# Scaling q and k on VectorE, the output gain moved to the gate, and another spread of the convolution taps

## The chip, the cores and the metric

The kernel runs on one core of one Trainium2 chip. The metric is the device time of the whole program in microseconds (us). Five engines matter: TensorE (PE in the rows: matmuls and transposes), VectorE (DVE), ScalarE (ACT), GpSimd (POOL) and the queue that issues the weight loads (SP). Each works through its own list of instructions in a fixed order, and waits on semaphores for the others.

## The reference

The reference is a stack of transformer blocks over 256 tokens of width 1024 in float32: two layers with attention and a convolution-gated feed-forward part, and then a block of another kind. The change touches the middle of that last block, a gated delta rule of 8 heads of 128 channels, which runs beside a long convolution:

```
c = depthwise_conv(glu_a * sigmoid(glu_b), conv_dw_w) + conv_dw_b          # 31 taps, 1024 channels
qkv = silu(depthwise_conv(concat(q, k, v), qkv_conv_w))                    # 5 taps
q = l2_norm(q) * (HEAD_DIM_2 ** -0.5)
k = l2_norm(k)
o_fwd = gated_delta_rule(q, k, v, g[:, :, 0], beta[:, :, 0])
o_bwd = rev(gated_delta_rule(rev(q), rev(k), rev(v), ...))
o = rms_norm(o_fwd + o_bwd, delta_norm_g) * silu(z)                        # gain of 128 numbers, the same for all heads
y_delta = o @ w_delta_out
```

## The kernel before

All weights are streamed from memory in slots of 1 MB. Each slot is split in two parts, a rounded one (whi, by ACT) and its remainder (wlo, by DVE or POOL), and every product is three matmuls on them (L981 to L983). That is most of TensorE's work.

The delta rule is laid out by hand as ten rounds of eight ticks. One half of a weight slot (24 matmuls, in two parts of 12) fills each tick for TensorE as long as the round has slots: rounds 0 to 5 have four (all eight ticks), round 6 three, round 7 two (ticks 0 to 3), round 8 three, round 9 four. Between these parts stand the steps of three heads at once: in round r the head r is prepared (its q, k and v), head r-1 has its triangular systems inverted, and head r-2 is finished.

- Inversion: ticks 1 to 6 each make one level. TensorE multiplies (L1318), DVE masks the product into `prod` (L2415), TensorE multiplies that (L1348, L1350), ACT copies the two results (L1806, L1808). L1318 stands at the start of the tick, L1348 behind the first 12 matmuls of the slot. Tick 7 is a check with L2421 in the place of L2415, and `solved` (L2433), for which TensorE waits at L1370.
- Preparation: in tick 3 TensorE turns q and k (L1261), and ACT takes four sums of squares (L1756). In tick 4 POOL makes reciprocal lengths of them (L919 twice, then the power L920), and ACT scales the four 128x128 pieces with them (L1761). In tick 5 TensorE turns them back (L1271). In tick 6 the decay ratios are started (L2383), in tick 7 they meet the products.
- Slots that end are evacuated by ACT and DVE at the start of the next even tick: for q, k and v eight taps of the short convolution (L2308, two groups of four around the other steps of the tick), for z the gate (`xn`, L2324), for the long convolution its input (L2319).
- The long convolution is 8 channel tiles of 31 taps each on DVE (L2363, L2368 and L2371), with a closing sum (`cacc`, L2375) for each tile. A table says how many taps each tick takes (`TAP_COUNT`: for even rounds 8, 6, 0, 5, 0, 3, 7, 4, for odd ones 8, 6, 0, 5, 3, 4, 6, 3). Half of a tick's taps stand before the steps of preparation, half behind.
- The halves of a slot's wlo that are made in ticks 4 and 5 are DVE's (L1989), the others POOL's (L939).

DVE's order within a tick is: `prod` of the level, evacuation part 0, the gate of the short convolution, taps part 0, the steps of preparation and finish, evacuation part 1, the wlo half, taps part 1.

The output's gain (`delta_norm_g_2`) is applied after round 9, when the outputs have been turned so that channels are rows: ACT multiplies by it while rounding (L1594, four times), and DVE does so for the remainders (L2025, four times).

## Time and profile before

| | |
|---|---|
| time, median of 3 runs | 1378.86 us (1376.05 to 1382.32) |
| the profiled execution | 1378.86 us, of which the span is 1377.0 |
| TensorE busy | 1322.1 us, 96% of the span |
| DVE busy | 860.5 us, 62% |
| ACT busy | 702.3 us, 51% |
| POOL busy | 194.2 us, 14% |
| mean granted TensorE clock | 0.982 |
| DMA, mean | 145 GB/s |

Shares are over the whole span. The stretch from the first decay values to the end of round 7 is 697 to 1010 us; in it TensorE is busy for 298.0 of 313 us, DVE for 240.1, ACT for 188.0. A row of the order of time gives start, length, engine, line, operation, tiles and shapes, count, and in brackets the idle time of the engine before it with what ended it. Rows with a count are merged, so that the length is from the first start to the last end. DVE's instructions overlap at their edges by about 0.08 us, so a length is that much longer than the step to the next one.

### The profile page before, as it was taken

The page shows a single profiled execution, that of the slowest core. Times are in us where ns is not written, and L with a number is a line of the kernel's source. Part 1 is how long each engine was busy: PE and PEld are TensorE (multiplying, and loading weights), DVE is VectorE, ACT ScalarE, POOL GpSimd, SP SyncE. Part 2 cuts the span into 40 slices and gives each one's busy share as a digit, 9 for nine tenths or more (in the row PEclk, how much of TensorE's full clock was granted, in tenths as well). Part 3 has the DMA queues.
Part 4 walks back from the last instruction along what each step waited for, and adds up shares of the span by engine and source line. Part 5 has one row for each costly group of instructions (what it writes and reads, how often), then busy time and mean ns, then how long its engine had stood idle before and what let it go on. Part 6 is the DMA issues. An engine that isn't in the chain of part 4 may idle for free.

```text
span 1377.0 us, 22043 instructions
## 1 busy us (share of the span) xinstructions
PE 1322.1 (96%) x9030; PEld 1207.6 (88%) x9030; DVE 860.5 (62%) x1468; ACT 702.3 (51%) x1154; POOL 194.2 (14%) x175
## 2 busy tenths in 40 slices
PE   8998999999999999999989999999888999999996
PEld 7776799998877799998889999999788989999875
DVE  6773578873654478885358787877734445555355
ACT  4553455553446555554266566666546335444343
POOL 2000000000000000000135535444422201000001
PEclk9998999999999999999999999999998999999998
DMA  7623155545433245555443233233102445455531
GB/s 278 232 98 121 64 196 185 184 163 191 173 132 123 80 149 185 184 184 188 155 149 123 93 123 101 84 123 123 62 31 93 168 153 189 170 189 183 183 137 74
DMA packets 31444, 200.32 MB, mean 145 GB/s; under 512 B 4272, under 2 KB 6464, under 8 KB 8560
## 3 DMA queue, kind: packets, MB, share of 16 engines
q1 hardware_dynamic: 29216, 189.26, 38.5%
q0 software_dynamic: 1984, 9.12, 1.9%
q8 instruction: 72, 1.18, 0.3%
q10 hardware_dynamic: 144, 0.52, 0.1%
q14 instruction: 28, 0.23, 0.1%
HBM read 197.85 MB, written 1.05 MB: 144 GB/s over the span
## 4 chain that ended last, share of the span: by engine, by line
PE 87%; DVE 7%; ACT 3%; issue 1%; DMA 1%; POOL 1%; SPq 0%; POOLq 0%; DVEq 0%; ACTq 0%
PE ps L981 25%; PE ps L982 24%; PE ps L983 24%; PE ps L1138 2%; PE ps L1348 2%; PE ps L1350 1%; PE ps L1106 1%; PE ps L1318 1%; DVE conv L2308 1%; DMA raw<-in_stream 1%; DVE wlo L1980 1%; PE ps L1119 1%; DVE xlo L2028 1%; DVE xn L2004 1%; PE ps L1289 1%
## 5 line engine op out<-in xcount | busy, mean ns | idle before, releaser
L981 PE MATMUL ps<-xhi,whi 128*128 128x256 f32 x1640 | 472.2, 288 | 5.8 <-DVE xlo L2025 2.6
L982 PE MATMUL ps<-xlo,whi 128*128 128x256 f32 x1640 | 465.8, 284 | 0.0
L983 PE MATMUL ps<-xhi,wlo 128*128 128x256 f32 x1640 | 465.6, 284 | 0.0
L1980 DVE TENSOR_TENSOR wlo<-raw,whi 128x2048 fp32r<-128x2048 f32 (+2 forms) x145 | 326.0, 2253 | 138.3 <-ACT whi L1552 134.2
L1552 ACT ACTIVATE whi<-raw 128x2048 fp32r<-128x2048 f32 (+2 forms) x145 | 271.5, 1879 | 130.9 <-PE ps L983 120.9
L981 PEld LDWEIGHTS ps<-xhi,whi 128*128 128x128 f32 x1640 | 315.7, 192 | 6.9 <-DVE xlo L2025 2.8
L982 PEld LDWEIGHTS ps<-xlo,whi 128*128 128x128 f32 x1640 | 315.9, 193 | 0.1
L983 PEld LDWEIGHTS ps<-xhi,wlo 128*128 128x128 f32 x1640 | 315.7, 192 | 0.1
L939 POOL TENSOR_TENSOR wlo<-raw,whi 128x1024 fp32r<-128x1024 f32 x54 | 130.0, 2425 | 104.9 <-ACT whi L1561 104.9
L874 POOL TENSOR_SCALAR sumsq<-sumsq 128x1 f32<-128x1 f32 x18 | 4.0, 222 | 850.9 <-ACT xn L1579 850.7
L981 PE MATMUL ps<-whi,xhi 128*128 128x512 f32 (+3 forms) x320 | 120.4, 376 | 3.5 <-DVE xlo L2028 3.0
L983 PE MATMUL ps<-whi,xlo 128*128 128x512 f32 (+3 forms) x320 | 115.9, 362 | 0.0
L982 PE MATMUL ps<-wlo,xhi 128*128 128x512 f32 (+3 forms) x320 | 115.6, 361 | 0.0
L981 PE MATMUL ps<-whi,hhi 128*128 128x512 f32 x264 | 104.3, 395 | 0.9 <-DVE hf L2253 0.9
L982 PE MATMUL ps<-wlo,hhi 128*128 128x512 f32 x264 | 105.0, 398 | 0.0
L983 PE MATMUL ps<-whi,hlo 128*128 128x512 f32 x264 | 103.8, 393 | 0.0
L1677 ACT ACTIVATE cv<-ps,par 128x256 f32<-128x256 f32 x88 | 45.0, 562 | 102.6 <-PE ps L983 102.6
L2371 DVE SCALAR_TENSOR_TENSOR ps<-glu_in,par,ps 128x256 f32<-128x256 f32 x224 | 94.8, 481 | 0.0
L1561 ACT ACTIVATE whi<-raw 128x1024 fp32r<-128x1024 f32 x72 | 75.8, 1056 | 9.2 <-PE ps L983 8.8
L981 PEld LDWEIGHTS ps<-whi,xhi 128*128 128x128 f32 x320 | 60.7, 190 | 18.5 <-issue 6.3
L983 PEld LDWEIGHTS ps<-whi,xlo 128*128 128x128 f32 x320 | 60.6, 189 | 9.5
L982 PEld LDWEIGHTS ps<-wlo,xhi 128*128 128x128 f32 x320 | 60.7, 190 | 8.0
(281 smaller groups left out, 1841.3 us busy)
## 6 DMA issues: line engine op xcount, KB each, us to landing
raw<-in_stream SPq DMA_DIRECT2D x176, 1024.0 KB, 4.8
gain<-in_gains POOLq DMA_DIRECT2D x8, 512.0 KB, 4.2
bias<-in_rel POOLq DMA_DIRECT2D x1, 1536.0 KB, 8.6
raw<-in_stream SPq DMA_DIRECT2D x2, 648.0 KB, 11.5
cst<-in_consts POOLq DMA_DIRECT2D x1, 1280.5 KB, 6.3
raw<-in_stream SPq DMA_DIRECT2D x2, 528.0 KB, 4.2
x<-in_x SPq DMA_DIRECT2D x2, 512.0 KB, 5.7
out<-xn SPq DMA_DIRECT2D x2, 512.0 KB, 2.6
```

The costliest lines, as they stand in the source:

```text
L939: pool.tensor_tensor(wlo[:, n % RING, c], raw[:, n % RAW, c], whi[:, n % RING, c].bitcast(F32), ALU.subtract).then_inc(*S["pool_weights_lo ...
L981: nc.tensor.matmul(out, a_hi, b_hi, start=start, stop=False)
L982: nc.tensor.matmul(out, a_hi, b_lo, start=False, stop=False)
L983: return nc.tensor.matmul(out, a_lo, b_hi, start=False, stop=stop)
L1106: last = nc.tensor.matmul(ps[:, 7, t * TOK + e % 4 * HD:t * TOK + (e % 4 + 1) * HD], probT[:, e % 2, (t + s_) * P:(t + s_ + 1) * P], v_of( ...
L1138: last = nc.tensor.matmul(ps[:, bank, tile_logits(t)], q, k, start=True, stop=True)
L1348: nc.tensor.matmul(ps[:, 5, y * P:(y + 1) * P], prod[:, y, :], inv_t[:, h % 2, y, :], start=True, stop=True)
L1552: act.activation(used(whi, n), used(raw, n), ACT.Copy).then_inc(*S["weights_high"].one((n, 1)))
L1561: act.activation(whi[:, n % RING, c], raw[:, n % RAW, c], ACT.Copy).then_inc(*S["weights_high"].one((n, half)))
L1677: act.activation(cv[:, j % 2, m, :], ps[:, j % 4, m * TOK:(m + 1) * TOK], ACT.Identity, bias=par_at(f"conv_b{li}", c), scale=par_at(f"conv ...
L1980: dve.tensor_tensor(used(wlo, n), used(raw, n), used(whi, n).bitcast(F32), ALU.subtract)\
L2371: dve.scalar_tensor_tensor(odd_taps[:, :] if k == 29 else sums, src, w, sums, ALU.mult, ALU.add)\
```

## The change

Three things are changed.

The scaling of q and k goes from ACT to DVE: four instructions of a 128x128 piece for each head, in tick 4, behind evacuation part 0 and taps part 0. The constant factors are a second scalar of the same instruction, so POOL needs one instruction before the power in place of two.

The gain of the output is multiplied into z's gate instead (two DVE instructions of 128x256 for each of the four z slots), so that it is gone from the rounding after round 9.

The taps of the long convolution are dealt out by a share of what is left (`TAP_SHARE`), in place of fixed counts.

```
-    c.add("delta_norm_g_2", inputs["delta_norm_g_2"][0].reshape(P, 1))
+        ("a_log_2", 0, 16), ("dt_bias_2", 0, 16), ("delta_norm_g_2", 0, 128)]
...
-TAP_COUNT = ([8, 6, 0, 5, 0, 3, 7, 4], [8, 6, 0, 5, 3, 4, 6, 3])
+TAP_SHARE = [5, 6, 0, 5, 0, 2, 4, 1, 5, 5, 0, 5, 2, 4, 3, 1]
...
+    share = [TAP_SHARE[tick % (2 * TICKS)] for tick in range(TICKS * 8)]
     for tick in range(TICKS * 8):
-        for _ in range(TAP_COUNT[tick // TICKS % 2][tick % TICKS]):
-            if todo and ready[todo[0][0]] < tick:
-                ticks.setdefault(tick, []).append(todo.pop(0))
+        most = -(-len(todo) * share[tick] // max(sum(share[tick:]), 1)) + (1 if share[tick] else 0)
+        while todo and most and ready[todo[0][0]] < tick:
+            ticks.setdefault(tick, []).append(todo.pop(0))
+            most -= 1
...
 (POOL, tick 4)
-                    for m in range(2):
-                        by = 4.0 * (P if m == 0 else 1)
-                        c = slice(m * TT, (m + 1) * TT)
-                        link(pool.tensor_scalar(qk_sq[:, c], qk_sq[:, c], 0.25 * by, EPS * by, ALU.mult, ALU.add))
+                    link(pool.tensor_scalar(qk_sq[:, :], qk_sq[:, :], 0.25, EPS, ALU.mult, ALU.add))
...
 (ACT, tick 4)
-                if i == 4:
-                    act.wait_ge(*S["qk_rstd_ready"].at(h))
-                    for y in range(4):
-                        act.activation(qk_tok[:, h % 2, y // 2, y % 2, :], ps[:, 2, y * P:(y + 1) * P], ACT.Copy,
-                                       scale=qk_rstd[:, y:y + 1]).then_inc(*S["qk_scaled"].one((h, y)))
...
 (DVE, tick 4)
+                if i == 4:
+                    dve.wait_ge(*S["qk_rstd_ready"].at(h))
+                    for y in range(4):
+                        scale = 0.5 * (P ** -0.5 if y < 2 else 1.0)
+                        dve.tensor_scalar(qk_tok[:, h % 2, y // 2, y % 2, :], ps[:, 2, y * P:(y + 1) * P],
+                                          qk_rstd[:, y:y + 1], scale, ALU.mult, ALU.mult).then_inc(*S["qk_scaled"].one((h, y)))
...
 (DVE, evacuation of z)
+                    dve.wait_ge(*S["tanh_used"].at(key))
+                    view = xn[:, :, c].rearrange("p t (h c) -> p t h c", h=2)
+                    for t in range(TT):
+                        last = dve.tensor_tensor(view[:, t, :, :], view[:, t, :, :],
+                                                 row_at["delta_norm_g_2"].unsqueeze(1).broadcast_to([P, 2, P]), ALU.mult)
+                    last.then_inc(*S["z_made"].one(key[1]))
...
 (after round 9: ACT and DVE)
-                                       ps[:, 4 + 2 * t + half, :].rearrange("p (i c) -> p i c", i=4), ACT.Copy,
-                                       scale=par_at("delta_norm_g_2", 0) if k == "o" else 1.0)\
+                                       ps[:, 4 + 2 * t + half, :].rearrange("p (i c) -> p i c", i=4), ACT.Copy)\
...
-                            ins = dve.scalar_tensor_tensor(xlo[at], src, par_at("delta_norm_g_2", 0), xhi[at].bitcast(F32),
-                                                           ALU.mult, ALU.subtract)
+                        dve.tensor_tensor(xlo[at], ps[:, 4 + 2 * t + half, :].rearrange("p (i c) -> p i c", i=4),
+                                          xhi[at].bitcast(F32), ALU.subtract).then_inc(*S["norm_low"].one((k, t, half)))
```

The order of TensorE's instructions is the same in both kernels. The taps per tick come out as follows, worked out from the two rules (ticks 0 to 7 of each round; 248 in all):

| round | before | sum | after | sum |
|---|---|---|---|---|
| 0 | 0 0 0 0 0 0 7 4 | 11 | 0 0 0 0 0 0 7 3 | 10 |
| 1 | 8 6 0 5 3 4 6 3 | 35 | 9 8 0 8 4 7 6 3 | 45 |
| 2 | 8 6 0 5 0 3 7 4 | 33 | 8 9 0 8 0 4 7 3 | 39 |
| 3 | 8 6 0 5 3 4 6 3 | 35 | 8 8 0 8 4 6 5 3 | 42 |
| 4 | 8 6 0 5 0 3 7 4 | 33 | 7 8 0 7 0 4 6 3 | 35 |
| 5 | 8 6 0 5 3 4 6 3 | 35 | 7 7 0 6 3 5 4 2 | 34 |
| 6 | 8 6 0 5 0 3 7 4 | 33 | 6 7 0 6 0 3 4 2 | 28 |
| 7 | 8 6 0 5 3 4 6 1 | 33 | 4 4 0 4 2 1 0 0 | 15 |

On DVE in tick 4 of round 2 (a round with a v slot; `conv` is the short convolution, `wlo` the remainders of a weight slot, `prod` the masked product of a level), before:

```order
L2415 TENSOR_TENSOR prod<-ps,cst 128x512
L2308 SCALAR_TENSOR_TENSOR conv<-ps,par,conv 128x254 x2
L2308 SCALAR_TENSOR_TENSOR conv<-ps,par,conv 128x255 x4
L2308 SCALAR_TENSOR_TENSOR conv<-ps,par,conv 128x254 x2
L1989 TENSOR_TENSOR wlo<-raw,whi 128x1024
L2415 TENSOR_TENSOR prod<-ps,cst 128x512
```

and of the changed kernel (its line numbers differ):

```order
L2416 TENSOR_TENSOR prod<-ps,cst 128x512
L2297 SCALAR_TENSOR_TENSOR conv<-ps,par,conv 128x254 x2
L2297 SCALAR_TENSOR_TENSOR conv<-ps,par,conv 128x255 x2
L2380 TENSOR_SCALAR qk_tok<-ps,qk_rstd 128x128 x4
L2297 SCALAR_TENSOR_TENSOR conv<-ps,par,conv 128x255 x2
L2297 SCALAR_TENSOR_TENSOR conv<-ps,par,conv 128x254 x2
L1983 TENSOR_TENSOR wlo<-raw,whi 128x1024
L2416 TENSOR_TENSOR prod<-ps,cst 128x512
```

The four scaling steps stand between the `prod` of tick 4 and that of tick 5. In tick 4 of round 1 (a round with a z slot there), DVE before:

```order
L2415 TENSOR_TENSOR prod<-ps,cst 128x512
L2324 SCALAR_TENSOR_TENSOR xn<-tanh,ps 128x2x256
L2371 SCALAR_TENSOR_TENSOR ps<-glu_in,par,ps 128x256
L2375 TENSOR_TENSOR cacc<-ps,odd_taps 128x256
L1989 TENSOR_TENSOR wlo<-raw,whi 128x1024
L2363 TENSOR_SCALAR ps<-glu_in,par,twice_b 128x256
L2368 TENSOR_SCALAR ps<-glu_in,par 128x256
L2415 TENSOR_TENSOR prod<-ps,cst 128x512
```

and of the changed kernel:

```order
L2416 TENSOR_TENSOR prod<-ps,cst 128x512
L2313 SCALAR_TENSOR_TENSOR xn<-tanh,ps 128x2x256
L2319 TENSOR_TENSOR xn<-xn,rows 128x256 x2
L2366 SCALAR_TENSOR_TENSOR ps<-glu_in,par,ps 128x256 x2
L2380 TENSOR_SCALAR qk_tok<-ps,qk_rstd 128x128 x4
L1983 TENSOR_TENSOR wlo<-raw,whi 128x1024
L2366 SCALAR_TENSOR_TENSOR ps<-glu_in,par,ps 128x256 x2
L2416 TENSOR_TENSOR prod<-ps,cst 128x512
```

Six instructions are added between the two `prod`, and the closing sum `cacc` has moved to tick 3. In tick 4 of round 7, where TensorE has no slot, DVE of the changed kernel has one tap on either side of the four scaling steps:

```order
L2416 TENSOR_TENSOR prod<-ps,cst 128x512
L2366 SCALAR_TENSOR_TENSOR ps<-glu_in,par,ps 128x256
L2380 TENSOR_SCALAR qk_tok<-ps,qk_rstd 128x128 x4
L2366 SCALAR_TENSOR_TENSOR odd_taps<-glu_in,par,ps 128x256
L2416 TENSOR_TENSOR prod<-ps,cst 128x512
```

where three taps stood before.

## Rows read from the trace of the kernel before

**Rows 1.** Busy time in rounds 1 and 2 (start:end, length, then each engine)

```profile
735.20:773.30 38.10, 37.32 (x312) 36.78 (x311) 31.53 (x73) 23.15 (x49) 19.53 (x13) 1.00 0.31 111
773.30:814.35 41.05, 39.85 (x335) 39.27 (x333) 32.51 (x75) 25.75 (x58) 18.52 (x14) 1.00 0.30 103
```

**Rows 2.** TensorE's waits from 700 to 1010 us: total, times, longest

```profile
PE ps L1348 <- DVE prod L2415: 5.7, 7, 0.9
...
PE ps L1370 <- DVE solved L2433: 2.4, 2, 1.6
...
PE ps L1279 <- DVE conv L2349: 0.8, 1, 0.8
```

**Rows 3.** In order of time, tick 4 to 5 of round 2, DVE and PE

```profile
791.54 3.22 DVE L2308 SCALAR_TENSOR_TENSOR conv<-ps,par,conv 128x254 f32<-128x254 f32 x8 [0.82 <-ACT conv L1719]
...
795.81 0.68 DVE L2415 TENSOR_TENSOR prod<-ps,cst 128x512 fp32r<-128x512 f32 x1
...
796.55 0.66 PE L1348 MATMUL ps<-inv_t,prod 128*128 128x128 f32 x4 [0.87 <-DVE prod L2415]
```

**Rows 4.** DVE groups by line: count, busy us, mean ns of one, idle before

```profile
L2390 DVE SCALAR_TENSOR_TENSOR upper<-ps,beta,ratio 128x128 f32<-128x128 f32 x32 | 9.0, 343 | 0.7 <-ACT ratio L1785 0.3
...
L2403 DVE TENSOR_TENSOR qk_ratio<-ps,ratio 128x256 f32<-128x256 f32 x16 | 6.0, 414 | 0.0
...
L2094 DVE COPY v<-ps 128x128 f32<-128x128 f32 x2 | 0.6, 284 | 0.0
...
L2025 DVE SCALAR_TENSOR_TENSOR xlo<-ps,par,xhi 128x512 fp32r<-128x512 f32 x4 | 2.7, 743 | 0.5 <-ACT xhi L1594 0.5
...
L2028 DVE TENSOR_TENSOR xlo<-ps,xhi 128x512 fp32r<-128x512 f32 x28 | 17.3, 681 | 0.0
```

**Rows 5.** In order of time, round 1, tick 4 to 5, DVE and PE

```profile
750.50 0.69 DVE L2415 TENSOR_TENSOR prod<-ps,cst 128x512 fp32r<-128x512 f32 x1 [1.39 <-PE ps L1318]
751.77 0.69 DVE L2324 SCALAR_TENSOR_TENSOR xn<-tanh,ps 128x512 f32<-128x512 f32 x1 [0.58 <-ACT tanh L1729]
...
755.21 0.68 DVE L2415 TENSOR_TENSOR prod<-ps,cst 128x512 fp32r<-128x512 f32 x1
...
755.99 0.61 PE L1348 MATMUL ps<-inv_t,prod 128*128 128x128 f32 x4
```

**Rows 6.** The same in round 3, tick 5

```profile
835.27 0.69 DVE L2415 TENSOR_TENSOR prod<-ps,cst 128x512 fp32r<-128x512 f32 x1
...
836.55 0.56 PE L1348 MATMUL ps<-inv_t,prod 128*128 128x128 f32 x4
```

**Rows 7.** Round 5, ticks 4 and 5, POOL and DVE

```profile
913.35 1.01 POOL L920 TENSOR_TENSOR qk_rstd<-qk_sq,half_power 128x4 f32<-128x4 f32 x1
...
913.57 1.23 DVE L1989 TENSOR_TENSOR wlo<-raw,whi 128x1024 fp32r<-128x1024 f32 x1
...
915.78 0.69 DVE L2415 TENSOR_TENSOR prod<-ps,cst 128x512 fp32r<-128x512 f32 x1 [0.19 <-PE ps L1318]
```

**Rows 8.** Round 7, ticks 4 and 5, POOL and DVE

```profile
991.01 0.48 POOL L919 TENSOR_SCALAR qk_sq<-qk_sq 128x2 f32<-128x2 f32 x2
991.58 1.01 POOL L920 TENSOR_TENSOR qk_rstd<-qk_sq,half_power 128x4 f32<-128x4 f32 x1
...
990.42 1.26 DVE L2371 SCALAR_TENSOR_TENSOR ps<-glu_in,par,ps 128x256 f32<-128x256 f32 x3
993.16 0.69 DVE L2415 TENSOR_TENSOR prod<-ps,cst 128x512 fp32r<-128x512 f32 x1 [1.48 <-PE ps L1318]
```

**Rows 9.** Round 6, tick 6, DVE, behind the start of the ratios

```profile
964.91 1.66 DVE L2371 SCALAR_TENSOR_TENSOR ps<-glu_in,par,ps 128x256 f32<-128x256 f32 x4
```

**Rows 10.** Two stretches; the third column from the right is the granted clock

```profile
700.00:712.00 12.00, 11.18 (x71) 11.00 (x71) 3.21 (x15) 7.06 (x11) 4.72 (x2) 0.74 0.41 167
960.00:972.00 12.00, 9.37 (x71) 8.46 (x70) 9.99 (x27) 6.32 (x15) 3.25 (x3) 1.00 0.24 87
```

**Rows 11.** POOL's wlo halves: least, median and longest in ns

```profile
L939 POOL TENSOR_TENSOR wlo<-raw,whi x54: 2346/2398/2662, 706.5 to 1079.6; 128x1024 fp32r<-128x1024 f32 x54
```

More of the change, by code:

```diff
@@ L244 @@
 ROWS = [("idx_k_ln_g", 0, 64), ("idx_k_ln_b", 0, 64), ("forget_b", 0, 8), ("sinks", 0, 8),
-        ("a_log_2", 0, 16), ("dt_bias_2", 0, 16)]
+        ("a_log_2", 0, 16), ("dt_bias_2", 0, 16), ("delta_norm_g_2", 0, 128)]
 def pack_gains(inputs):
@@ L257, in param_places @@
     shapes = {"ffn_conv_w": (2, 3, 2 * FF), "ffn_conv_b": (2, 2 * FF), "qkv_conv_w_2": (1, 5, 3 * D), "conv_dw_w_2": (1, 31, D),
-              "conv_dw_b_2": (1, D), "conv_ln_g_2": (1, D), "conv_ln_b_2": (1, D), "delta_norm_g_2": (1, P)}
+              "conv_dw_b_2": (1, D), "conv_ln_g_2": (1, D), "conv_ln_b_2": (1, D)}
     empty = {name: np.zeros(shape, np.float32) for name, shape in shapes.items()}
@@ L359 @@
     "qk_squared": "sum of squares, (h, 2 * m + t)",
-    "qk_rstd_ready": "reciprocal lengths times the factors of q and k, h",
+    "qk_rstd_ready": "reciprocal lengths, h",
     "qk_scaled": "normalized q or k, (h, 2 * m + t)",
@@ L403 @@
     "tanh_used": "the doubled product with the sigmoid is written",
+    "z_made": "z's silu times the gain in xn, pair of heads",
     "slot_read_act": "tanh of both gates is written",
@@ L560 @@
 TANH_OF, TANH_BEFORE, LAST_TANH = tanh_order()
-TAP_COUNT = ([8, 6, 0, 5, 0, 3, 7, 4], [8, 6, 0, 5, 3, 4, 6, 3])
+TAP_SHARE = [5, 6, 0, 5, 0, 2, 4, 1, 5, 5, 0, 5, 2, 4, 3, 1]
 def tap_schedule():
     ready = {key[1]: r * TICKS + tick + 1 for key, r, tick in MIX_SLOTS if key[0] == "glu"}
-    ticks, todo = {}, [(j, k) for j in range(KT) for k in range(31)]
+    ticks, todo, n = {}, [(j, k) for j in range(KT) for k in range(31)], 0
+    share = [TAP_SHARE[tick % (2 * TICKS)] for tick in range(TICKS * 8)]
     for tick in range(TICKS * 8):
-        for _ in range(TAP_COUNT[tick // TICKS % 2][tick % TICKS]):
-            if todo and ready[todo[0][0]] < tick:
-                ticks.setdefault(tick, []).append(todo.pop(0))
+        most = -(-len(todo) * share[tick] // max(sum(share[tick:]), 1)) + (1 if share[tick] else 0)
+        while todo and most and ready[todo[0][0]] < tick:
+            ticks.setdefault(tick, []).append(todo.pop(0))
+            most -= 1
     assert not todo
@@ L2022, in lows @@
                         at = (slice(None), slice(4 * half, 4 * half + 4), slice(t * P, (t + 1) * P))
-                        src = ps[:, 4 + 2 * t + half, :].rearrange("p (i c) -> p i c", i=4)
-                        if k == "o":
-                            ins = dve.scalar_tensor_tensor(xlo[at], src, par_at("delta_norm_g_2", 0), xhi[at].bitcast(F32),
-                                                           ALU.mult, ALU.subtract)
-                        else:
-                            ins = dve.tensor_tensor(xlo[at], src, xhi[at].bitcast(F32), ALU.subtract)
-                        ins.then_inc(*S["norm_low"].one((k, t, half)))
+                        dve.tensor_tensor(xlo[at], ps[:, 4 + 2 * t + half, :].rearrange("p (i c) -> p i c", i=4),
+                                          xhi[at].bitcast(F32), ALU.subtract).then_inc(*S["norm_low"].one((k, t, half)))
             def add_quarter_to_x(k, n):
@@ L2450, in finish @@
                     dve.wait_ge(*S["o_rstd_ready"].at(h))
-                    dve.wait_ge(*S["tanh_used"].at(("z", h // 2)))
+                    dve.wait_ge(*S["z_made"].at(h // 2))
                     for t in range(TT):
```

## The prediction

> **What bounds the kernel now.** I read four things in turn. The table: TensorE is busy for 96% of the span, so a microsecond counts only if it makes TensorE wait or takes a wait away. The busy time by round: round 1 lasts 38.10 us with DVE busy for 31.53, round 2 lasts 41.05 with 32.51 [rows 1], so DVE has 6.6 and 8.5 us of idle time in a round, and it looks as if there were room for more work there. TensorE's waits in the delta rule: 5.7 us for `prod` in seven places, 2.4 us for `solved` in two, 0.8 us for the gate of the short convolution in one [rows 2]. These 8.9 us are all that DVE costs TensorE from 700 to 1010 us. Last the order of time, because it tells where DVE's idle time lies: in front of the `prod` of a level, where it waits for TensorE's product. That is time that DVE can't use for what stands behind it in the list. What counts is how late DVE comes to the next `prod`, tick by tick.
>
> The measure for that: where TensorE does wait, it starts L1348 0.74 us after `prod` has started (795.81 to 796.55 in [rows 3]). So the slack of a `prod` that isn't waited for is the start of its L1348, less 0.74, less its own start. In tick 5 of round 1 it is 755.99 - 0.74 - 755.21 = 0.04 us [rows 5], in tick 5 of round 3 836.55 - 0.74 - 835.27 = 0.54 us [rows 6], and where DVE has been waiting for the product in a tick with a slot (as in rounds 3 and 5) it is the same 0.54. In tick 5 of the even rounds there is none left.
>
> **What the new instructions take.** A DVE instruction of 128x128 with one operand in PSUM lasts 343 ns, less 0.08 for the overlap, so steps of 0.26 us [rows 4]; four scaling steps are 1.04 us. The trace has no tensor_scalar of this form. From below: a copy from PSUM of this size takes 284 ns, in steps of 0.20, which makes 0.8 us. From above: no overlap at all, 4 x 343 ns = 1.4 us. I take 1.04, for that row also reads a scalar for each partition. Two instructions of 128x256 last 414 ns each, in steps of 0.33 [rows 4], with the overlap at the end 0.75 us; that is what I take for z's gain, with 0.66 below and 0.83 above. A tap is a step of 0.39 us (three last 1.26 us in [rows 8], eight of nearly the same form 3.22 in [rows 3]).
>
> The trace shows that an instruction with one operand in PSUM is not quicker for having a single tensor to read: the copy is only 59 ns below the three-operand form [rows 4]. The Trainium skill ("VectorE: DVE Perf Modes", section "Why PSUM operands drop a tier") says that fp32 with any PSUM operand runs at one element a cycle, where SBUF operands of a tensor_scalar would run at two. By it the four steps have no quick form, as I assume; if they had one, the first rival below would come true.
>
> **Even rounds (v slots): 0, 2, 4, 6.** In tick 4 DVE waits 0.82 us for ACT, does the eight taps of the short convolution, the wlo half, and then `prod`, for which TensorE is already waiting 0.87 us [rows 3]. The scaling steps go between the fourth and the fifth of the eight. The reciprocal lengths should be there: in round 7 they will be ready 1.9 us behind the end of tick 4's `prod` (990.42 to 992.31, below), and here the fourth of the eight ends 0.82 + 1.6 = 2.4 us behind it. Nothing between the start of the eight and `prod` is idle, so the 1.04 us pass to TensorE whole. In round 0 there is no level, but the same chain ends at the gate for which TensorE waits 0.8 us [rows 2]. Four rounds: 4 x 1.04 = 4.2 us. The extra taps in tick 3 of rounds 2 and 4 (three and two, some 1.2 and 0.8 us) vanish in the 0.82 us that DVE waits for ACT and in the idle time before the `prod` of tick 4.
>
> **Odd rounds with z in tick 4: 1 and 3.** DVE gets 0.75 for the gain and 1.04 for scaling. In round 1 the taps of the tick go from three to four, but the closing sum moves to tick 3, -0.2 together; in round 3 +0.39. DVE comes late to the `prod` of tick 5 by 1.6 and 2.2 us; less the slack of 0.04 and 0.54, TensorE waits 1.6 us in each: 3.2 us. The 0.58 us of idle time in tick 4 is a wait for ACT's tanh in front of the new instructions [rows 5], and hides only what comes late from tick 3: three more taps and there, in round 1, the sum, 1.7 us against 1.39 of idle time before the `prod`.
>
> **Round 5.** Here DVE meets the wait that the change adds, for POOL's power. It ends at 913.35 + 1.01 = 914.36 [rows 7]; with one small POOL instruction less it is 0.28 us earlier (two of them and the steps to the power take 991.58 - 991.01 = 0.57 us [rows 8]), 914.08. Behind this wait stand the wlo half, two taps and the `prod` of tick 5. The wlo half began at 913.57 and now would begin at 914.08 + 1.04 = 915.12, 1.55 us later; DVE had 0.19 us idle before the `prod` [rows 7], slack is 0.54: TensorE waits 0.8 us.
>
> **Round 7.** No slot in ticks 4 to 7, so TensorE runs from product to product and any lateness shows. Power ready at 991.58 + 1.01 - 0.28 = 992.31 [rows 8], scaling until 993.35, one tap 0.39, `prod` at 993.74 and not at 993.16: 0.6 us. The 18 taps fewer in this round bring nothing, since DVE was idle for 1.48 us before that `prod` [rows 8]: it waited for TensorE, not TensorE for taps.
>
> **What comes back.** In tick 6 of round 6, four taps stand between the ratios and the check [rows 9], and behind them two in tick 7, on the way to `solved`, for which TensorE waits 1.6 us [rows 2]. Three of these six go, 1.2 us at most; ACT's exponentials, which run beside them, then become the last, so I take 0.5 (0.4 at least, the tap of tick 7). After round 9 the four remainders lose 743 - 681 = 62 ns each [rows 4], 0.25 us. ACT loses eight times four steps, but no wait of TensorE in [rows 2] names ACT. The table's other taps (9 and 8 in ticks 0 and 1 of rounds 1 to 3) meet idle time before the next `prod`.
>
> Sum: 4.2 + 3.2 + 0.8 + 0.6 - 0.5 - 0.25 = 8.0 us. The profiled execution took 1378.86 us, the same as the median of the three runs, with its span 1377.0; so I forecast 1387 us, a span of about 1385. By the bounds of the scaling steps, used in eight rounds, it is 2 us less or 3 more; z's gain adds 0.2 either way.
>
> **Rivals.**
> 1. *The additions fit into DVE's idle time.* For it: 6.6 and 8.5 us a round [rows 1] against some 1.0 of scaling, at most 0.8 to 1.5 of gain and up to 3.9 of taps. Against it: the even rounds' chain has no gap. With scaling at 0.2 a step and the odd rounds' lateness halved, 8.0 - 1.7 - 1.6 = 4.7 us: 1383.5, no change that can be told.
> 2. *The lighter end of the table gives more than the scaling takes.* 24 taps (9.4 us of DVE) leave rounds 5 to 7. If TensorE's waits for `solved` (2.4 us) and the last four of the seven for `prod` in ticks without a slot (about 0.8 us each, 3.2) were DVE's load and went, and DVE's new work were hidden, the time is 1378.9 - 5.6 - 0.25 = 1373 us. It decides if more than about 5 us of those waits are load. Against it: DVE stood idle 1.48 us before one of them [rows 8].
> 3. *DVE's taps spill over in rounds 1 to 3.* If slack is smaller than I read it, the 8 or 9 taps of ticks 0, 1 and 3 make nine more `prod` late by a tap, 0.39 us: 3.5 us, 1390.5.
> 4. *GpSimd and DVE get in each other's way.* POOL's wlo half takes 2398 ns at the median and 2662 at most [rows 11], so something holds it for 0.26 us at times. DVE's new gain is the kind of instruction that may be held in turn: at four places, from 0 to a whole half of 2.4 us each, and on the path in two to four of them. With half of that at four, 4.8 us: 1392. The Trainium skill ("SBUF — State Buffer", "Who interferes with whom") states it as a lock: a DVE instruction with two inputs in SBUF and a GpSimd instruction that reads SBUF exclude each other, and the later one waits for the whole of the other. The trace's 0.26 us on POOL agrees; a DVE instruction that waits for POOL it doesn't show.
> 5. *The new waits cost TensorE its clock.* From 700 to 712 us the granted clock was 0.74, so part of it was at 1.2 GHz and not 2.4; at a TensorE that was busy this lost 0.26 x 12 = 3.1 us. If six waits of 1.6 us or more did that, 19 us: 1406. Against it: from 960 to 972 us TensorE was busy for only 9.37 of 12 us and the clock stayed at 1.00 [rows 10].
>
> **Chances and range.** Forecast 0.50; rival 1 0.21; rival 2 0.07; rivals 3 and 4 together 0.18; rival 5 0.04. The likeliest case's own range is 1384 to 1390. About 0.5% (6.9 us, 1372.0 to 1385.8) is what a measurement can tell from no change. Of the forecast's half about 0.10 falls below 1385.8, with all of rival 1 and 0.02 of rival 2: no change 0.33. Faster 0.05, slower 0.62. The range 1378 to 1396 takes in the cases 1, 3 and 4 and leaves out 2 and 5 and the ends of 4.
>
> **What the changed profile would show.** TensorE's wait at the L1348 of tick 5 in rounds 2, 4 and 6: 1.9 us and not 0.87; at L1279 in round 0, 1.8 and not 0.8; new waits of 1.6 us at tick 5 of rounds 1 and 3, 0.8 in round 5; from 700 us on the sum of waits for `prod` up from 5.7 to about 13. DVE's scaling steps 0.26 us apart, ACT's busy time 8 us less, the round 7 as long as before within a microsecond although DVE has 7 us less to do. I am wrong if the waits for `prod` in even rounds stay at 0.9 (then scaling was hidden), if round 7 gets shorter, or if the clock falls between 712 and 990 us.

## The result, and the profile after

| | before | after |
|---|---|---|
| median of the timed runs | 1380.46 us (1376.05 to 1382.32) | 1397.96 us (1393.24 to 1398.95) |
| ratio, 95% interval | | 1.014 (1.0112 to 1.0169) |
| profiled execution | 1378.86 us, span 1377.0 | 1398.52 us, span 1396.7 |
| granted clock over the span | 0.982 | 0.979 |

The change makes the kernel slower by 17.5 us in the medians and 19.7 us in the profiled pair. The forecast was 1387 us, 8 us slower. What follows takes the profiled pair apart; single executions of the changed kernel lay between 1393 us at a mean clock of 0.982 and 1403 us at 0.974, and that spread turns out to be part of the answer.

The table of the page of the changed kernel, busy time and number of instructions:

```profile
PE 1328.4 (95%) x9030; PEld 1213.4 (87%) x9030; DVE 877.0 (63%) x1508; ACT 693.6 (50%) x1122; POOL 193.0 (14%) x167
```

TensorE has the same 9030 matmuls. First where the time goes, by round: each stretch runs from the start of tick 0 to the start of the next (start:end, length, busy time of PE, PEld, DVE, ACT and POOL with the number of instructions, then the granted clock, the DMA share and GB/s). Rounds 1 to 4 of the kernel after:

```profile
736.29:777.47 41.18, 38.89 (x311) 38.15 (x310) 36.61 (x88) 22.11 (x45) 19.15 (x12) 0.96 0.29 103
777.47:819.51 42.04, 39.79 (x335) 39.22 (x333) 35.99 (x85) 24.72 (x54) 18.32 (x13) 1.00 0.29 101
819.51:866.39 46.88, 42.78 (x331) 42.00 (x329) 39.30 (x86) 23.46 (x51) 18.85 (x13) 0.93 0.25 91
866.39:912.05 45.66, 41.86 (x335) 40.96 (x333) 38.76 (x88) 24.82 (x54) 18.64 (x13) 0.96 0.26 93
```

Rounds 1, 3 and 4 of the kernel before, between the same marks (round 2 is in [rows 1]; its row for round 1 is 0.2 us longer):

```profile
735.23:773.15 37.92, 37.14 (x310) 36.60 (x309) 31.35 (x73) 23.15 (x49) 19.35 (x13) 1.00 0.31 112
814.18:853.66 39.48, 39.15 (x331) 38.78 (x329) 31.55 (x73) 24.49 (x55) 18.84 (x14) 1.00 0.31 108
853.66:894.69 41.03, 39.83 (x334) 39.26 (x333) 32.84 (x76) 25.75 (x58) 18.51 (x14) 1.00 0.30 103
```

Round 2 is 1.0 us longer, as forecast for it. Round 1 is 3.3 us longer (1.6 forecast), round 3 7.4 (1.6 forecast) and round 4 4.6 (1.0 forecast). Two marks stand in these rows: the granted clock is below 1.00 in rounds 1, 3 and 4 and in none of these rounds was before, and DVE is busy 7.8 us longer in round 3 for 13 more instructions, where steps of 0.3 to 0.4 us would make 5.

TensorE's waits from 700 to 1020 us, total, times and longest, kernel after; they answer to [rows 2]:

```profile
PE ps L1348 <- DVE prod L2416: 13.3, 10, 1.9
PE ps L1376 <- DVE rest L2443: 3.9, 2, 2.3
...
PE ps L1279 <- DVE conv L2344: 1.8, 1, 1.8
PE ps L1370 <- DVE solved L2434: 1.5, 1, 1.5
```

The sum for `prod` is the "about 13" that the prediction named. The second row is new: the prediction has no wait for `rest`. Third, the stretches around three of the waits, and the one behind a fourth (columns as above), kernel after:

```profile
757.00:760.00 3.00, 1.49 (x13) 1.31 (x12) 3.00 (x8) 0.16 (x1) 0.00 (x0) 1.00 0.00 0
760.50:764.00 3.50, 3.50 (x19) 3.50 (x18) 2.63 (x6) 1.78 (x4) 0.00 (x0) 0.51 0.58 178
821.00:825.00 4.00, 1.99 (x16) 1.79 (x16) 4.00 (x10) 0.69 (x1) 2.81 (x2) 1.00 0.50 209
825.40:828.80 3.40, 3.40 (x17) 3.40 (x18) 3.40 (x9) 1.45 (x4) 0.00 (x0) 0.50 0.78 299
846.00:849.20 3.20, 1.68 (x14) 1.58 (x14) 3.06 (x8) 0.43 (x1) 0.00 (x0) 1.00 0.02 5
849.30:852.70 3.40, 3.40 (x18) 3.40 (x17) 2.71 (x6) 1.54 (x5) 0.00 (x0) 0.50 0.30 70
873.20:876.61 3.41, 3.41 (x18) 3.41 (x18) 2.02 (x6) 1.83 (x5) 0.00 (x0) 0.50 0.55 228
```

In each pair TensorE waits for DVE in the first stretch and then runs without a gap at a granted clock of a half, 1.2 GHz and not 2.4. The last row is the fourth such stretch, 1.7 us behind the wait of 1.66 us for `rest` in round 4. Each lasts 3.41 us in which half the clock is gone: 1.7 us. This text calls such a stretch a fall.

So the 19.7 us of the profiled pair are three sums: 7.9 us of waits that were forecast, 3.9 us of waits for `rest`, and 4 x 1.7 = 6.8 us of clock. The other 1.1 us lie in pieces of 0.1 to 0.3 us in most rounds and have not been followed.

All executions on record bear this out in sum. A span times one minus its mean granted clock is a rough measure of the time lost to the lower clock, and the remainder is the span without it (the clock is given to three places, so one execution's split is good to 0.7 us; a mean is better). Over 29 executions of the changed kernel the remainder is 1365.8 us on average (1363.2 to 1367.7) and the loss 31.5; over 70 executions of the kernel before, 1353.8 and 23.8. So 12.0 us of the difference don't depend on the clock, against 11.8 us of waits counted above, and 7.7 us on average are clock.

### The profile page after: what moved, and what is told of

It is laid out like the page before. It is cut to its first block, busy times and chain, and to the rows that moved or that the text cites. A ratio compares the mean times of both kernels' runs of the same rounds, so it can differ in the third digit from the quotient of the medians.

```text
span 1396.7 us, 22043 instructions
## 1 busy us (share of the span) xinstructions
PE 1328.4 (95%) x9030; PEld 1213.4 (87%) x9030; DVE 877.0 (63%) x1508; ACT 693.6 (50%) x1122; POOL 193.0 (14%) x167
## 3 DMA queue, kind: packets, MB, share of 16 engines
HBM read 197.92 MB, written 1.05 MB: 142 GB/s over the span
## 4 chain that ended last, share of the span: by engine, by line
PE 82%; DVE 10%; ACT 3%; POOL 2%; issue 1%; DMA 1%; SPq 0%; POOLq 0%; DVEq 0%; ACTq 0%
PE ps L981 23%; PE ps L982 23%; PE ps L983 22%; PE ps L1138 2%; PE ps L1348 1%; PE ps L1106 1%; PE ps L1350 1%; DVE conv L2297 1%; PE ps L1318 1%; DVE xlo L2017 1%; DVE ps L2366 1%; DMA raw<-in_stream 1%; DVE wlo L1974 1%; DVE wlo L1983 1%; PE ps L1119 1%
```

## Experiments

Times are medians; ratios are to the kernel before on the same chip (medians 1380.5 to 1380.9), with 95% intervals. "Falls" are those of 3.41 us between 712 and 990 us of the profiled execution. A longer stretch at half clock (7 to 14 us) begins in round 7 of every kernel, at 992.89 before and at 988.57 at the earliest (the last kernel of the table); it isn't counted. The last two columns are the split by the clock, in means over all executions, less the same for the kernel before on that chip (for the changed kernel, in the first line, over all 70).

| kernel | time, us | ratio | falls | waits of TensorE of 1.5 us or more, 712 to 990 | span without lost clock | lost clock |
|---|---|---|---|---|---|---|
| after | 1397.96 | 1.014 (1.0112 to 1.0169) | 4 | 8 | +12.0 | +7.7 |
| taps alone | 1377.59 | 0.997 (0.9956 to 0.9984) | 0 | 0 | -0.7 | -3.0 |
| scaling alone | 1387.07 | 1.0045 (1.0029 to 1.0061) | 1 | 5 | +7.6 | -1.7 |
| gain alone | 1388.15 | 1.0056 (1.0036 to 1.0076) | 2 | 3 | +4.9 | +3.8 |
| after, gain in PSUM | 1390.83 | 1.0073 (1.0049 to 1.0098) | 2 | 6 | +9.3 | +1.1 |
| after, POOL behind the gain | 1390.36 | 1.0081 (1.0061 to 1.0100) | 2 | 6 | +8.3 | +3.0 |
| after, waits filled | 1401.87 | 1.0145 (1.0118 to 1.0172) | 0 | 1 | +20.4 | -0.1 |
| after, waits half filled | 1393.32 | 1.0092 (1.0071 to 1.0113) | 0 | 1 | +13.1 | +0.4 |
| scaling, wlo half late | 1380.72 | 1.001 (0.9994 to 1.0025) | 0 | 1 | +0.7 | +0.9 |
| after, gain in PSUM and wlo half late | 1385.18 | 1.004 (1.0026 to 1.0055) | 0 | 0 | +3.7 | +2.4 |
| taps, wlo half late | 1376.41 | 0.9976 (0.9960 to 0.9992) | 0 | 0 | -2.5 | -0.7 |
| taps, wlo half late in even rounds | 1374.98 | 0.9968 (0.9954 to 0.9982) | 0 | 0 | -3.8 | -0.8 |

### One part of the change at a time

Taps alone: `TAP_SHARE` on the kernel before.

```
-TAP_COUNT = ([8, 6, 0, 5, 0, 3, 7, 4], [8, 6, 0, 5, 3, 4, 6, 3])
+TAP_SHARE = [5, 6, 0, 5, 0, 2, 4, 1, 5, 5, 0, 5, 2, 4, 3, 1]
...
```

> The kernel before with the new spread of the taps alone. Theory (what counts is lateness at the next prod; the taps meet idle time in front of it): no change, 1380 us within 2, TensorE's waits for prod within 0.3 us of before in every round, the granted clock at 1.00 from 712 to 990 us. Rival (the taps are what makes DVE late in rounds 1 to 3 of the changed kernel): waits for prod or rest appear in rounds 1 to 4, 1384 us or more.

Measured 1377.59 us, a little faster, and 0.4 us below the range expected. In rounds 1 to 5 the waits are those of before within 0.1 us; round 6 is 0.57 us shorter. So the taps are not a cause; they pay in the place and nearly the size (0.5) that the prediction gave them. The rest of the 3.3 us in the medians is mostly clock (3.0 us less lost than in the runs beside it).

Scaling alone (with GpSimd's single instruction, as in the change):

```
-   act.activation(qk_tok[...], ps[:, 2, y * P:(y + 1) * P], ACT.Copy, scale=qk_rstd[:, y:y + 1])
+   dve.tensor_scalar(qk_tok[...], ps[:, 2, ...], qk_rstd[:, y:y + 1], scale, ALU.mult, ALU.mult)
```

> The kernel before with the scaling of q and k on DVE alone (with POOL's single instruction). Theory: each scaling step is 0.26 us on DVE's list; TensorE's waits grow by 1.04 us in rounds 0, 2, 4 and 6, by 1.0 in round 1, 0.5 in round 3, 0.8 in round 5 and 1.0 in round 7, 7.4 us together, 1388 us, and the clock stays at 1.00 from 712 to 990 us since no odd round has a wait of 1.5 us. Rival (the clock falls behind any of these waits, 1.9 us in even rounds): one to five falls of 3.41 us at half clock, 1.7 us each, 1390 to 1396 us.

Measured 1387.07 us. Waits from 700 to 1020 us of this kernel:

```profile
PE ps L1345 <- DVE prod L2413: 12.3, 10, 2.0
```

12.3 us for `prod`, 5.7 before. Behind one of the three waits of 1.90 us the clock fell:

```profile
800.94:804.35 3.41, 3.41 (x19) 3.41 (x17) 1.30 (x3) 1.27 (x3) 0.00 (x0) 0.50 0.47 166
```

The time is the theory's; its clock without a fall is not, and the rival's fall came once.

Gain alone, the multiplies in z's gate (and the gain gone from the roundings behind round 9):

```
+   for t in range(TT):
+       last = dve.tensor_tensor(view[:, t, :, :], view[:, t, :, :], row_at["delta_norm_g_2"]..., ALU.mult)
```

> The kernel before with one part of the change: the output gain multiplied into z's gate (two VectorE multiplies of 128x256 in each of the four z slots), and gone from the roundings behind round 9. The taps and the scaling stay as before. Theory (the gain itself costs little, GpSimd's shares of the next weights hold it): in tick 0 of rounds 3 and 4 one of the two multiplies takes about 2.6 us instead of 0.42, the rest is late, and TensorE waits about 2 us in round 3 and 1.5 us in round 4; in rounds 1 and 3 the multiplies of tick 4 make prod of tick 5 late by about 0.7 and 0.2 us; about 0.3 us comes back behind round 9. That is 4 to 4.5 us, and each fall of the clock behind one of these waits adds 1.7 us, one to three of them: 1386 to 1389 us against 1380.5 before. Rival (the 4 x 0.75 us of the multiplies alone count, nothing is held): no wait above 1 us in rounds 3 and 4, and 1380 to 1382 us.

Measured 1388.15 us. From 712 to 990 us TensorE waits, in this kernel,

```profile
PE ps L1376 <- DVE rest L2442: 4.2, 2, 2.2
PE ps L1348 <- DVE prod L2415: 4.0, 5, 0.9
```

and in order of time one sees why (DVE, tick 0 of round 3):

```profile
814.03 3.21 DVE L2324 TENSOR_TENSOR xn<-xn,rows 128x256 f32<-128x256 f32 x2
```

3.21 us for two instructions of 0.42. The theory came true, the wait of round 4 was longer than expected (2.04), and the clock fell behind both. By ratios the three parts are -4.1, +6.2 and +7.7 us: together 9.8, less than the 15 to 23 us of the whole. In the profiled spans they are -1.2, +9.5 and +9.4: 17.7 of 19.7. Medians and profiles differ here because the clock lost differs from one execution to the next. With the lost clock taken off, the parts are -0.7, +7.6 and +4.9 us, 11.8 together, against 12.0 for the whole: they add up. Their lost clock doesn't (-0.9 together against +7.7): in the profiled executions the whole has eight waits of 1.5 us or more and four falls, where the parts have none, five and three waits, with no, one and two falls.

### What holds the gain: GpSimd

Timeline of POOL and of DVE in tick 0 of rounds 3 and 4, kernel after:

```profile
816.48 4.96 POOL L939 TENSOR_TENSOR wlo<-raw,whi 128x1024 fp32r<-128x1024 f32 x2
...
818.79 2.93 DVE L2319 TENSOR_TENSOR xn<-xn,rows 128x256 f32<-128x256 f32 x2
...
863.20 4.92 POOL L939 TENSOR_TENSOR wlo<-raw,whi 128x1024 fp32r<-128x1024 f32 x2
...
864.80 3.60 DVE L2319 TENSOR_TENSOR xn<-xn,rows 128x256 f32<-128x256 f32 x2
```

The eight multiplies of the line, least, median and longest in ns:

```profile
L2319 DVE TENSOR_TENSOR xn<-xn,rows x8: 420/426/2590, 753.5 to 865.8; 128x256 f32<-128x256 f32 x8
```

Taken one by one, the multiplies of round 4 and the second POOL instruction beside them:

```profile
864.80 1.09 DVE L2319 TENSOR_TENSOR xn<-xn,rows 128x256 f32<-128x256 f32 x1
865.82 2.59 DVE L2319 TENSOR_TENSOR xn<-xn,rows 128x256 f32<-128x256 f32 x1
...
865.56 2.57 POOL L939 TENSOR_TENSOR wlo<-raw,whi 128x1024 fp32r<-128x1024 f32 x1
```

The first POOL instruction ended at 865.61 and the second at 868.13; the multiplies ended 0.28 us behind each, at 865.89 and 868.41. In round 3 the second multiply ends 0.3 us behind the second POOL instruction in the same way. In tick 4 of round 3 POOL is busy too, with the power of the reciprocal lengths, but holds nothing:

```profile
842.11 1.01 POOL L920 TENSOR_TENSOR qk_rstd<-qk_sq,half_power 128x4 f32<-128x4 f32 x1
...
842.47 0.77 DVE L2319 TENSOR_TENSOR xn<-xn,rows 128x256 f32<-128x256 f32 x2
```

So it is POOL's long subtraction that matters, and not any POOL instruction. Two experiments take this apart: one leaves POOL alone and gives the multiply a single operand in SBUF, the other leaves the multiply alone and moves POOL.

Gain in PSUM:

```
+   part = src[:, t * TOK:(t + 1) * TOK]...                       # z's product, still in PSUM
+   last = dve.tensor_tensor(part, part, row_at["delta_norm_g_2"]..., ALU.mult)
    dve.scalar_tensor_tensor(xn[:, :, c], tanh..., 1.0, src..., ALU.add, ALU.mult)
```

> The changed kernel, with z's gain multiplied in place in PSUM ahead of the gate, so that its two instructions have one input in SBUF and not two; their number, shape and place are the same. Theory (they were held by POOL's wlo halves in tick 0 of rounds 3 and 4): they last 0.4 us each and none 2.59; TensorE's waits for rest at L1376 in rounds 3 and 4 (2.25 and 1.66 us) go, with the clock falls behind them; 3.9 + 3.4 = 7.3 us less than the changed kernel, 1391 us. Rival (DVE is late there by its additional taps and instructions): these waits stay, 1397 us.

Measured 1390.83 us. The same place, and POOL beside it:

```profile
815.92 4.74 POOL L939 TENSOR_TENSOR wlo<-raw,whi 128x1024 fp32r<-128x1024 f32 x2
...
817.53 0.75 DVE L2315 TENSOR_TENSOR ps<-ps,rows 128x256 f32<-128x256 f32 x2
```

POOL behind the gain (GpSimd's program):

```
+   behind = finished_slot(r + 1, 0) if i == 7 and r + 1 < len(ROUNDS) else None
+   if behind and behind[0] == "z":
+       pool.wait_ge(*S["z_made"].at(behind[1]))
    if slot_at(r, i):
        split_half(slot_of[slot_at(r, i)] + AHEAD, i % 2)
```

> The changed kernel; the only edit is a wait on GpSimd: its half of the next weights that used to run beside z's gain in tick 0 of rounds 3 and 4 starts only when that gain is done. The two multiplies still read two operands from SBUF. Theory (GpSimd's running subtraction holds a VectorE multiply with two operands in SBUF): both multiplies take 0.42 us again, the waits of 2.25 and 1.66 us on rest are gone, and so are the clock falls behind them (3.4 us): 1390 to 1391 us, as with the gain in PSUM, against 1398. Rival (it is the second operand in SBUF, or this place, that makes the multiply slow, whatever GpSimd does): a multiply of 2.6 us stays and the time stays at 1397 to 1399 us. Second rival (the weights are late when GpSimd starts 2 to 3 us later): the waits on rest go, a wait on wlo of 1 us or more comes in ticks 1 or 2 of rounds 3 and 4, and the time is above 1393 us.

Measured 1390.36 us. DVE in tick 0 of round 3:

```profile
816.02 0.76 DVE L2322 TENSOR_TENSOR xn<-xn,rows 128x256 f32<-128x256 f32 x2
```

and POOL:

```profile
816.86 7.06 POOL L939 TENSOR_TENSOR wlo<-raw,whi 128x1024 fp32r<-128x1024 f32 x3 [3.12 <-DVE xn L2322]
```

With the same operands and POOL waiting for 3.12 us, the pair is back at 0.76; both waits for `rest` are gone, and nobody waits for the later weights. Either side's absence is enough, so the cause is the meeting of a two-SBUF-operand DVE instruction and POOL's subtraction. By the medians this is 7.1 to 7.6 us of the loss, waits and clock together. The Trainium skill ("SBUF — State Buffer", "Who interferes with whom") calls it an exclusive lock; by that rule the later of the two waits for the whole of the other. The trace agrees for the subtraction, with 2.59 us against 0.42; for the power of 128x4 (0.43 and 0.42 us beside it) it doesn't show a hold.

### What the waits cost besides their length: the clock

Idle matmuls ahead of the new waits, whose results nobody uses:

```
+   FILL5, FILL1 = {0: 12, 1: 15, 2: 12, 3: 15, 4: 5, 5: 15}, {1: 18, 2: 13}
...
+   if i == 5:
+       spin(FILL5.get(h, 0), 5)
    pe.wait_ge(*S["prod_made"].at((h, i)))
...
+       spin(FILL1.get(h, 0), 5)
    pe.wait_ge(*S["rest_made"].at(h))
```

The keys are heads: `FILL5` fills tick 5 of rounds 1 to 6, `FILL1` tick 1 of rounds 3 and 4.

> The changed kernel, with idle matmuls of 128 columns on TensorE ahead of its waits for prod in tick 5 of rounds 1 to 6 and for rest in tick 1 of rounds 3 and 4, a little fewer than fill the waits. Theory (TensorE's waits cost it the clock, on top of their length): DVE's times are the same, the granted clock is 1.00 from 712 to 990 us, and the time is 4 falls of 1.7 us less, 1391 us. Rival (the falls have another cause, or the extra time isn't the clock): 1398 us, or more by what the matmuls overrun.

Measured 1401.87 us. The clock stayed at 1.00 from 712 to 990 us, but the experiment was badly sized: an idle matmul takes twice what I had reckoned, so 12 to 18 of them overran the waits and cost more than the falls. The split shows both: no more clock lost than before the change (-0.1 us), and 8.4 us more without it than in the changed kernel. With half as many (`FILL5 = {0: 6, 1: 8, 2: 6, 3: 7, 4: 2, 5: 8}`, `FILL1 = {1: 9, 2: 6}`; the text below says rounds 0 to 5 for what are rounds 1 to 6):

> The changed kernel with idle 128x128 matmuls put on TensorE ahead of the six waits on tick 5's prod (6, 8, 6, 7, 2 and 8 of them in rounds 0 to 5) and of the two waits on tick 1's rest (9 in round 3, 6 in round 4), half as many as in the run before, so that they end inside the waits. Their results are not used. Theory (the rests of the loss are falls of the granted clock behind the waits): the waits become matmuls of the same length, the clock stays at 1.00 from 712 to 990 us, and the four stretches at half clock, 1.7 us each, are gone: 1391 to 1392 us against 1398 of the changed kernel. Rival (the falls are chance of one execution, the waits alone carry the loss): 1397 to 1399 us.

Measured 1393.32 us (lowest 1386.98), 1.3 us above the range expected; the profiled execution, 1391.68, is within it. Busy time and clock of the whole stretch:

```profile
712.00:990.00 278.00, 269.58 (x2231) 264.04 (x2229) 234.00 (x536) 155.63 (x339) 122.33 (x78) 1.00 0.28 102
```

and the filled wait of round 3 in order of time:

```profile
821.25 2.17 PE L991 MATMUL ps<-ident 128*128 128x128 f32 x18
823.66 0.71 PE L1382 MATMUL ps<-rest,solved 128*128 128x128 f32 x4 [0.24 <-DVE rest L2449]
```

DVE is about as late as in the changed kernel: 2.17 us of idle matmuls (nine, two records each) and 0.24 us of wait stand where 2.25 us of wait stood. What differs is that TensorE was busy. The profiled span is 1389.8 us, 6.9 us less than after: the four falls of 1.7 us. What is left over the kernel before, 12.8 us, is the forecast's 8 and the 3.9 for `rest`, but for 0.9 us. The medians show a smaller gain (4.6 us), but they are of four and six executions, and the clock lost differs between executions. In the means over all 29 and 6, the loss of clock goes from 7.7 to 0.4 us above that of the kernel before, while the rest grows by 1.1 (12.0 to 13.1): filling the waits takes the clock's part away and leaves the rest.

### What makes the even rounds pay: the wlo half in front of `prod`

The VectorE half of the low-order weights of tick 4 stands between the convolution's taps and `prod`. Postponed behind `prod` and the gate:

```
+LATER = [(r, 4) for r in range(HEADS)]
...
+   if (r, i - 1) in LATER and slot_at(r, i - 1):
+       split_half(slot_of[slot_at(r, i - 1)] + AHEAD, 0)
    long_taps(r * TICKS + i, 0)
...
-   if slot_at(r, i):
+   if slot_at(r, i) and (r, i) not in LATER:
```

First on the scaling alone:

> The kernel before with the scaling of q and k on VectorE, and with the VectorE half of the low-order weights of tick 4 postponed behind prod and the gate of tick 5. Output gain and taps stay as before. Theory (the scaling costs by standing in front of prod and by nothing else): the waits in tick 5 of rounds 2, 4 and 6 fall from 1.90 to about 0.8 us, that of round 0 from 1.8 to about 0.6, those of rounds 1, 3 and 5 from about 0.7 to nothing: some 6.7 us less than the scaling alone (1387), 1380 to 1381 us, and no fall of the clock in rounds 0 to 6. Rival (the scaling costs by itself, or the lateness only moves to tick 6): 1385 to 1387 us.

Measured 1380.72 us, where the scaling alone was 1387.07. DVE in round 2:

```profile
792.62 1.12 DVE L2380 TENSOR_SCALAR qk_tok<-ps,qk_rstd 128x128 f32<-128x128 f32 x4
793.66 1.64 DVE L2303 SCALAR_TENSOR_TENSOR conv<-ps,par,conv 128x255 f32<-128x255 f32 x4
795.22 0.68 DVE L2416 TENSOR_TENSOR prod<-ps,cst 128x512 fp32r<-128x512 f32 x1
```

The four scaling steps are there, 1.12 us, and the kernel is level with the one before, with the waits of rounds 2, 4 and 6 at 0.76 and those of rounds 1, 3 and 5 gone; only that of round 0 stayed, at 1.45 (0.6 expected). This is a trade and doesn't make the scaling free: with the half late and no scaling (below) round 2 has no such wait and lasts 40.05 us, here 40.92. The scaling still costs what stands in front of a `prod` that is waited for; what came back is what the half had cost there.

The whole change with both mends, gain in PSUM and the half late:

> The whole change, with z's gain multiplied in PSUM and VectorE's half of the low-order weights of tick 4 postponed behind prod and the gate of tick 5. Theory (two causes and their clock falls make up the loss): against 1390.8 us with the gain in PSUM, 1.1 us less in each of rounds 2, 4 and 6, 0.9 in rounds 1 and 3, 0.7 in round 5, 0.35 in round 0, which is 6.2 us, and the two clock falls left, 3.4 us: 1381 to 1385 us, level with or just above the kernel before. Rival (the change has a cost of its own that neither mend takes away): 1387 us or more.

Measured 1385.18 us, 0.2 us above the upper end of the theory. The clock is 1.00 from 712 to 990 us. From there TensorE still waits, more often and less long:

```profile
PE ps L1351 <- DVE prod L2419: 5.7, 8, 1.0
```

In rounds 1 and 3 the gate's two multiplies and the postponed half push tick 5 (0.37 us each) and then tick 6 (0.72 and 1.04). So the mended change is still slower than before; this part I had not forecast.

The same postponement without scaling and gain, on the taps alone:

> The kernel before with the change's division of the taps alone, and in addition the VectorE half of the low-order weights of tick 4 postponed in every round behind prod and the gate of tick 5. Scaling and output gain stay as before. Theory (what is in front of prod in tick 5 is what TensorE waits for): the waits of 0.87 us in rounds 2, 4 and 6 and that of 0.76 us in round 0 go, 3.4 us together: 1374 to 1375 us against 1377.6 with the taps alone. Rival (the postponed half is then late for the next user of the weights, or the lateness comes up one tick later): 1377 us or more, with a new wait of 0.3 us or more in tick 5 or 6.

Measured 1376.41 us, short of the theory, and its rival was partly right: rounds 2 and 4 are 1.0 us shorter each than with the taps alone, but rounds 1 and 3, where nothing had waited, are 0.5 and 0.8 us longer, with new waits. Tick 6 of round 1 and of round 3:

```profile
759.68 0.66 PE L1354 MATMUL ps<-inv_t,prod 128*128 128x128 f32 x4 [0.27 <-DVE prod L2421]
...
840.05 0.66 PE L1354 MATMUL ps<-inv_t,prod 128*128 128x128 f32 x4 [0.60 <-DVE prod L2421]
```

Postponed in even rounds alone, `LATER = [(r, 4) for r in range(0, HEADS, 2)]`:

> The kernel before with the change's division of the taps, and VectorE's half of the low-order weights of tick 4 postponed behind prod and the gate of tick 5 in rounds 0, 2, 4 and 6 alone. Theory (the postponement paid in the even rounds, 1.0 us in each of rounds 2 and 4, and cost 0.5 and 0.9 us in rounds 1 and 3, where TensorE had not been waiting and the postponed half now stands ahead of a later prod): 1.3 us less than with all rounds postponed (1376.4), so 1375 us. Rival (the two losses belong to the even rounds' postponement, carried over): 1376 to 1377 us, with the waits of 0.27 and 0.60 us in rounds 1 and 3 as they were.

Measured 1374.98 us, as expected, and the lowest median here: 0.9968 (0.9954 to 0.9982) of the kernel before. The intervals of the three kernels with the taps overlap (0.9970, 0.9976, 0.9968), so by the ratios they can't be told apart; without lost clock they are -0.7, -2.5 and -3.8 us, and the profiled rounds agree, with rounds 1 and 3 back at their old length and rounds 2 and 4 at 40.05 us. From 700 to 1010 us TensorE waits for `prod` four times, 3.3 us, where it had waited seven times, 5.7 us; from 712 to 960 us once:

```profile
PE ps L1324 <- ACT inv L1808: 2.4, 6, 0.8
PE ps L1354 <- DVE prod L2421: 1.0, 1, 1.0
PE ps L1285 <- DVE conv L2355: 0.4, 1, 0.4
```

## Why the prediction was wrong

The sign was right, the size was not: 8 us against 17.5 (19.7 in the profiled pair). Step by step.

**The sum of 8.0 us came out.** DVE and PE in order of time in round 2, after, against [rows 3]:

```profile
797.41 1.12 DVE L2380 TENSOR_SCALAR qk_tok<-ps,qk_rstd 128x128 f32<-128x128 f32 x4
...
801.14 0.68 DVE L2416 TENSOR_TENSOR prod<-ps,cst 128x512 fp32r<-128x512 f32 x1
...
801.88 0.66 PE L1348 MATMUL ps<-inv_t,prod 128*128 128x128 f32 x4 [1.92 <-DVE prod L2416]
```

| term | forecast | measured |
|---|---|---|
| even rounds 0, 2, 4, 6 | 4.2 | 1.04 + 1.05 + 0.94 + 1.05 = 4.1 |
| rounds 1 and 3, tick 5 | 3.2 | 1.51 + 1.52 = 3.0 |
| round 5 | 0.8 | 0.74 |
| round 7 | 0.6 | 1.54 - 0.78 = 0.76 |
| round 6, `solved` and the check | -0.5 | -0.14 - 0.25 = -0.4 |
| behind round 9 | -0.25 | -0.3 |
| sum | 8.0 | 7.9 |

The rows of rounds 1, 3, 5 and 7 (these answer to [rows 5 to 8]):

```profile
758.70 0.66 PE L1348 MATMUL ps<-inv_t,prod 128*128 128x128 f32 x4 [1.51 <-DVE prod L2416]
...
847.62 0.55 PE L1348 MATMUL ps<-inv_t,prod 128*128 128x128 f32 x3 [1.52 <-DVE prod L2416]
...
935.27 0.66 PE L1348 MATMUL ps<-inv_t,prod 128*128 128x128 f32 x4 [0.74 <-DVE prod L2416]
...
1013.35 0.69 PE L1348 MATMUL ps<-inv_t,prod 128*128 128x128 f32 x2 [1.54 <-DVE prod L2416]
```

and that of round 7 before:

```profile
993.91 1.11 PE L1348 MATMUL ps<-inv_t,prod 128*128 128x128 f32 x4 [0.78 <-DVE prod L2415]
```

The measure of slack (start of L1348, less 0.74, less the start of `prod`) held in every round, and a scaling step took 0.34 us in steps of 0.26, the value that I took. One reading was incomplete: the 8.9 us are not "all that DVE costs TensorE from 700 to 1010 us", since waits of 0.8 us for `decay` and 0.25 us for the check's `prod` stand there too. The sum doesn't use them, but the 0.25 went with the taps and is in the table above.

**The step that failed first: "with the overlap at the end 0.75 us; that is what I take for z's gain, with 0.66 below and 0.83 above".** The bounds came from DVE instructions with an operand in PSUM. The gain reads two operands in SBUF, and in two of its four slots, in tick 0 of rounds 3 and 4, POOL's subtraction was running: 2.93 and 3.60 us, not 0.75. The sum has no term for these two slots at all. At 0.75 that would have been right, for with POOL moved nobody waits there. I had the mechanism as rival 4 (half a POOL instruction held at four places, 4.8 us, 1392) but left it out of the sum and shared 0.18 between it and rival 3. The order of instructions with POOL's rows beside it would have told which slots meet it: the z slots evacuated in tick 0 do, those in tick 4 do not. The price was near: 3.9 us of waits for `rest`, two places and not four.

**The step that failed second: "Against it: from 960 to 972 us TensorE was busy for only 9.37 of 12 us and the clock stayed at 1.00".** One stretch in which the clock did not fall was read as a sign that it would not fall behind waits of this length. Over all thirteen profiled executions, 32 waits of 1.5 us or more (one of them 1.495) stand between 712 and 990 us, and 11 of them had a fall within 2 us behind them; no shorter wait had one. [Rows 10] was one of the 21 others. My price for rival 5 was wrong too: six times 3.1 us, from a stretch that held most of two falls. Measured is 1.7 us each, four times. With what these runs show, the chance of 0.04 at 1406 us would have been an expectation: eight new or longer waits of 1.5 us or more, some third of them with a fall of 1.7 us, 4 to 5 us in the likeliest case.

**The two errors feed each other.** Each wait for `rest` is also one more wait that can cost the clock, and did. Gain in PSUM took 7.1 us away in the medians, of which 3.9 are the two waits in the profile.

**Rivals.** 1 (the additions fit in) fell: all waits came. 2 (the lighter end gives more) fell in size: 0.4 to 0.6 us. 3 (taps spill over) fell: with the taps alone nothing waits more. 4 and 5 were both true beside the forecast; I had treated as alternatives what adds up.

**What would have shown me wrong:** "if the clock falls between 712 and 990 us". It did.

**Open.** Which of the long waits is followed by a fall isn't settled: behind the 1.92 us of round 2 the clock stayed in the changed kernel and fell with scaling alone. It differs between executions, as the times from 1393 to 1403 us with clocks of 0.982 to 0.974 show. That the clock goes with the waits is shown by filling them; why it falls behind a third of them and not behind the others is not.

## What to carry to other kernels

Before moving work to VectorE, sort its new instructions by where the operands are, and lay GpSimd's rows beside them: an instruction with two SBUF operands can cost what is left of a long GpSimd instruction (here 2.4 us of subtraction; a power of 128x4 cost nothing). Where TensorE is 95% busy, price a new wait by its length plus a chance of a clock fall, and ask how many waits become long rather than how long they are in sum. And if a wait is made by what stands in front of one instruction, reorder there first: postponing 1.2 us of work that nobody was waiting for gave back as much as the scaling had cost (1387.07 to 1380.72 us), and helped in the even rounds without the scaling too. In rounds 1 and 3, where nothing had waited, it made new waits.
